# Low part of the dense activations ahead of the next split, and constant products between the steps of the routers' choice

## The reference

```python
def swiglu(h, w_gate_up, w_down):
    g, u = jnp.split(h @ w_gate_up, 2, axis=-1)
    return (jax.nn.silu(g) * u) @ w_down

def moe_swiglu(h, w_router, b_router, w_gate_up, w_down):
    ...
    logits = (hf @ w_router).astype(jnp.float32) + b_router.astype(jnp.float32)
    top_v, top_i = lax.top_k(logits, TOP_K)
    top_w = jax.nn.softmax(top_v, axis=-1)
    gates = jnp.sum(jax.nn.one_hot(top_i, N_EXPERTS, dtype=jnp.float32) * top_w[..., None], axis=1)
    ...
```

## Time and profile before

| | |
|---|---|
| median of 3 runs | 1820.67 us (1820.63 to 1828.91) |
| profiled execution | 1822.73 us |
| its span, first to last instruction | 1821.2 us |
| mean granted TensorE clock | 0.978 of full speed |
| PE busy | 1734.4 us, 95% |
| DVE busy | 1278.9 us, 70% |
| ACT busy | 998.8 us, 55% |
| POOL busy | 246.8 us, 14% |
| first dense layer | about 155 to 358 us |
| second dense layer | about 1050 to 1241 us |
| routers' choice | about 491 to 500 us and 1387 to 1396 us |

### The profile page before, as it was taken

The page is one execution under the profiler, slowest core; times in us unless marked ns, Lnnn a source line. Parts: engine busy times, 40 slices in busy tenths (PEclk is TensorE's granted clock), DMA queues, the critical chain, the costliest instruction groups (busy, mean ns, idle before and its releaser), DMA issues. The chain is left out here.

```text
span 1821.2 us, 26440 instructions
## 1 busy us (share of the span) xinstructions
PE 1734.4 (95%) x10773; PEld 1594.1 (88%) x10773; DVE 1278.9 (70%) x1245; ACT 998.8 (55%) x883; POOL 246.8 (14%) x294
## 2 busy tenths in 40 slices
PE   7989999899899999999999999999988999999997
PEld 7969899789789999999878999998976999999996
DVE  5567888774569888888866454446425788888887
ACT  5364343333457777777644354334463777777774
POOL 4838950000000000000210000000020000000010
PEclk9999999989999999999999999999998999999999
DMA  7526786654269998998943045444513799999984
GB/s 290 206 76 246 254 284 216 231 215 151 106 237 360 353 368 353 347 350 356 383 149 139 35 182 195 144 174 176 194 47 117 277 343 365 354 367 353 363 353 175
DMA packets 53756, 450.12 MB, mean 247 GB/s; under 512 B 6768, under 2 KB 8976, under 8 KB 16928
## 3 DMA queue, kind: packets, MB, share of 16 engines
q1 hardware_dynamic: 48480, 430.40, 62.4%
q0 software_dynamic: 5184, 18.40, 2.7%
HBM read 427.67 MB, written 21.10 MB: 246 GB/s over the span
## 5 line engine op out<-in xcount | busy, mean ns | idle before, releaser
L365 DVE TENSOR_TENSOR wlo<-raw,whi 128x3072 fp32r<-128x3072 f32 (+1 forms) x278 | 854.6, 3077 | 299.5 <-ACT whi L358 298.7
L358 ACT ACTIVATE whi<-raw 128x3072 fp32r<-128x3072 f32 (+1 forms) x278 | 706.2, 2541 | 412.0 <-PE PS L315 398.6
L313 PE MATMUL PS<-wlo,hT_hi 128*128 128x384 f32 (+2 forms) x1936 | 627.5, 324 | 6.2 <-DVE hT_lo L1976 3.4
L314 PE MATMUL PS<-whi,hT_lo 128*128 128x384 f32 (+2 forms) x1936 | 624.3, 322 | 0.0
L315 PE MATMUL PS<-whi,hT_hi 128*128 128x384 f32 (+2 forms) x1936 | 624.3, 322 | 0.0
L313 PEld LDWEIGHTS PS<-wlo,hT_hi 128*128 128x128 f32 x1936 | 367.4, 190 | 12.1 <-DVE hT_lo L1976 4.1
L314 PEld LDWEIGHTS PS<-whi,hT_lo 128*128 128x128 f32 x1936 | 367.4, 190 | 3.2 <-issue 0.2
L315 PEld LDWEIGHTS PS<-whi,hT_hi 128*128 128x128 f32 x1936 | 367.4, 190 | 0.3
L313 PE MATMUL PS<-wlo,mhi 128*128 128x512 f32 x352 | 143.7, 408 | 2.4 <-DVE mlo L1989 2.4
L315 PE MATMUL PS<-whi,mhi 128*128 128x512 f32 x352 | 139.1, 395 | 0.0
L314 PE MATMUL PS<-whi,mlo 128*128 128x512 f32 x352 | 139.1, 395 | 0.0
(11 more groups left out here) (372 smaller groups left out, 2021.3 us busy)
## 6 DMA issues: line engine op xcount, KB each, us to landing
raw<-in_weights SPq DMA_DIRECT2D x203, 1536.0 KB, 7.2
raw<-in_weights SPq DMA_DIRECT2D x73, 1024.0 KB, 6.2
raw<-s_tables SPq DMA_DIRECT2D x8, 1536.0 KB, 7.5
expert_rows<-ysb POOLq DMA_DIRECT2D x14, 512.0 KB, 6.8
s_tables<-g_out SPq DMA_DIRECT2D x8, 640.0 KB, 3.8
t_af<-s_rows_af SPq DMA_DIRECT2D x32, 128.0 KB, 3.8
s_tables<-g_out SPq DMA_DIRECT2D x8, 512.0 KB, 4.6
raw<-in_weights SPq DMA_DIRECT2D x3, 1152.0 KB, 5.5
```

Of the source, the lines that this page charges most:

```text
L313: pe.matmul(o, sh, mlw, start=start, stop=False, skip_group_check=True)
L314: pe.matmul(o, sl, mh, start=False, stop=False, skip_group_check=True)
L358: act.activation(whi[p0 % SPL][:, 0:n], raw[p0 % RAW][:, 0:n], ACT.Copy).then_inc(hi_done, 1)
L365: dve.tensor_tensor(wlo[p0 % SPL][:, 0:n], raw[p0 % RAW][:, 0:n], whi[p0 % SPL][:, 0:n].bitcast(F32), ALU.subtract).then_inc(lo_done, 1)
```

## The change

In `dense_act`, ScalarE makes the high part of the last activations ahead of its last split (piece u7 + 3) instead of behind it. In `dense_dve`, VectorE makes the low part of step j - 1 at the head of step j, ahead of the split of piece g + 3 instead of behind it, and at the end of the layer ahead of the split of piece u7 + 3 and of the last taps. The taps of the other steps keep their place. In `moe_pe`, TensorE issues two constant products into bank 1 behind the transposes of the logits, and one behind the counts.

```diff
@@ -1021,37 +1021,43 @@
                         .then_inc(f_hi, 1)
                 if 2 <= j < JD:
                     split_hi(act, b0 + ND["d", j - 2] + SPL)
-                if j < JD:
+                if j < JD - 1:
                     split_hi(act, b0 + ND["u", j] + SPL)
+                elif j == JD:
+                    split_hi(act, b0 + ND["u", JD - 1] + SPL)
 
         def dense_dve(dve, f, n):
             b0 = base[f"dense{f}"]
-            for j in range(JD + 2):
-                if 1 <= j <= JD:
-                    m = GU_D[j - 1][1] // P * L
-                    if j < JD:
-                        split_lo(dve, b0 + ND["g", j] + SPL)
-                    dve.wait_ge(f_hi, JD * f + j)
-                    dve.tensor_tensor(ALO[(j - 1) % 2][:, 0:m], psf[:, turn_at(j):turn_at(j) + m],
-                                      AHI[(j - 1) % 2][:, 0:m].bitcast(F32), ALU.subtract).then_inc(f_lo, 1)
-                elif j == 0:
-                    split_lo(dve, b0 + ND["g", j] + SPL)
-                if f == 0 and 1 <= j < KC:
+            def low_part(j):
+                m = GU_D[j][1] // P * L
+                dve.wait_ge(f_hi, JD * f + j + 1)
+                dve.tensor_tensor(ALO[j % 2][:, 0:m], psf[:, turn_at(j + 1):turn_at(j + 1) + m],
+                                  AHI[j % 2][:, 0:m].bitcast(F32), ALU.subtract).then_inc(f_lo, 1)
+
+            for j in range(JD):
+                if f == 0 and j >= 2:
+                    s5_taps_dve(dve, j - 1)
+                if j >= 1:
+                    low_part(j - 1)
+                split_lo(dve, b0 + ND["g", j] + SPL)
+                if f == 0 and j >= 1:
                     s5_powers_dve(dve, j)
-                if 2 <= j < JD:
+                if j >= 2:
                     split_lo(dve, b0 + ND["d", j - 2] + SPL)
-                if j < JD:
-                    p, w = b0 + ND["u", j], GU_D[j][1]
-                    dve.wait_ge(w_used, p + 1)
-                    dve.wait_ge(f_silu, JD * f + j + 1)
-                    for t in range(TT):
-                        i = dve.scalar_tensor_tensor(out=ff["act"][:, t, 0:w], in0=PS[:, 2 + t, 0:w],
-                                                     scalar=stat[:, 2, t:t + 1], in1=ff["sg"][:, t, 0:w],
-                                                     op0=ALU.mult, op1=ALU.mult)
-                    i.then_inc(f_mul, 1)
+                p, w = b0 + ND["u", j], GU_D[j][1]
+                dve.wait_ge(w_used, p + 1)
+                dve.wait_ge(f_silu, JD * f + j + 1)
+                for t in range(TT):
+                    i = dve.scalar_tensor_tensor(out=ff["act"][:, t, 0:w], in0=PS[:, 2 + t, 0:w],
+                                                 scalar=stat[:, 2, t:t + 1], in1=ff["sg"][:, t, 0:w],
+                                                 op0=ALU.mult, op1=ALU.mult)
+                i.then_inc(f_mul, 1)
+                if j < JD - 1:
                     split_lo(dve, p + SPL)
-                    if f == 0 and 1 <= j < KC:
-                        s5_taps_dve(dve, j)
+            low_part(JD - 1)
+            split_lo(dve, b0 + ND["u", JD - 1] + SPL)
+            if f == 0:
+                s5_taps_dve(dve, JD - 1)
             for half in range(2):
                 c = slice(half * 512, half * 512 + 512)
                 for t in range(TT):
@@ -1672,6 +1678,7 @@
             for t in range(TT):
                 last = pe.transpose(PS[:, 5, t * NE:(t + 1) * NE], mo["lgt"][:, t * P:(t + 1) * P], ident[0:NE, 0:NE])
             last.then_inc(m_pe, 1)
+            keep_warm(pe, 1, 2)
 
             pe.wait_ge(m_dve, 3 * m + 3)
             sel = mo["sel"]
@@ -1681,6 +1688,7 @@
                 .then_inc(m_pe, 1)
             pe.matmul(PS[:, 3, 0:NE], ones, sel[:, 0, :], start=True, stop=False, skip_group_check=True)
             pe.matmul(PS[:, 3, 0:NE], ones, sel[:, 1, :], start=False, stop=True, skip_group_check=True)
+            keep_warm(pe, 1, 1)
 
             def gather(e):
                 g = NE * m + e
```

## The result

The changed kernel took 1808.84 us, median of 7 runs (1807.88 to 1816.22), against 1820.67 us for the kernel before in 7 runs of the same comparison (1815.74 to 1828.91). The ratio is 0.9948, 95% interval 0.9925 to 0.9971, which is 9.5 us faster with 5.3 to 13.7 as the interval. The profiled execution took 1812.86 us, its span is 1811.3 us, and the mean granted clock 0.986.

The account below looks back on a forecast made before the run. TensorE, with matmuls covering 95% of the span, was taken as the bound, so only its ended stalls count: 4.5 + 2.8 + 1.0 + 0 = 8.3 us off 1820.67 gives 1812.4 us, range 1807.7 to 1817.

Parts of the forecast that it names:

- Part 1: Step 2 of the first dense layer: low part ahead of the gate split ends TensorE's idle and half-speed stretch, 4.5 us.
- no wait of TensorE for `alo` in either dense layer: Sign that the forecast is right: TensorE never waits for the activations' low part in the two dense layers.
- near 25.7 us: Sign that the forecast is right: the time from turns to turns in step 2 of the first dense layer.
- `alo` of step 2 is done at 205.6: First dense layer: VectorE finishes the low part 1.2 us before TensorE asks, everything behind being 0.7 us later.
- rival (a): VectorE is late in the stretch shared with GpSimd; the 4.5 us shrink to nothing at worst, 1816.9 us; chance 0.15.
- Part 2: End of the first dense layer: TensorE finishes 7.4 us sooner, but VectorE's queue becomes the bound, so 2.8 us arrive.
- fourth place of the queue at 351.7: End of the first dense layer: VectorE's split ends at 347.7, its table products at 351.7, then the adds to x.
- Part 3: End of the second dense layer: TensorE's wait of 0.98 us for the low part behind one split goes, 1.0 us.
- Part 4: Constants in the routers' choice: gather at full clock, but VectorE's two splits cover it and gate piece stays low; nothing.
- Rival (b): S5 begins at the low clock after 4.6 us of idle; constants take 1.9 us more, 1814.3 us; chance 0.14.
- Rival (c): Router constants hold the clock into the first gate piece, 1.5 us twice, 1809.4 us; chance 0.12.
- Rival (d): Slower: waiting for ScalarE's high part makes VectorE the bound beside GpSimd, 1834 us at worst; chance 0.04.

Follow-up runs that it names:

- e9: Changed kernel with GpSimd making only two of its eight groups of S5 tables; only times up to 350 us read: step 2 took 25.73 us.
- e3: Kernel before with the new order in the steps of both dense layers only, old order at the ends, no constants: 1815.49 us, ratio 0.9991.
- e4: Kernel before with the new order at the ends of both dense layers only, old order in the steps, no constants: 1814.73 us, ratio 0.9976.
- e8: Changed kernel with the first dense layer's last table products behind the adds to x, their store behind two table loads: 1809.51 us, ratio 0.9937.
- e2: Kernel before with only the three constant calls of each router added: 1820.97 us, ratio 1.0001.
- e1: Changed kernel without its constant calls in the routers: 1810.55 us, ratio 0.9953 to the kernel before.
- e5: Changed kernel run again without an edit: 1810.89 us, ratio 0.9947 to the kernel before.
- e10: Changed kernel with four more constant calls behind the transposes of expert 0's tokens: 1807.54 us, ratio 0.9938 to the kernel before.
- e12: Changed kernel without its own three constant calls, but with four behind the transposes of expert 0's tokens: 1809.35 us, ratio 0.9952.
- e7: Changed kernel with the first dense layer's step 1 table products moved behind the low part of step 2: 1812.14 us, ratio 0.9951.
- e6: Changed kernel with five more constant calls ahead of the norm behind the first dense layer and four ahead of expert 0's gate product: 1808.52 us, ratio 0.9936.

## Why the prediction was right

The time came out at 1808.84 us, 3.6 us under the forecast of 1812.4. It is inside the range of 1807.7 to 1817, but 0.7 us outside the narrower one of 1809.5 to 1815 that the forecast was given for itself. The three parts were named rightly, and their sum of 8.3 us was 0.8 us too high by the traces, which would make 1813.2. That the kernel came out faster than that is no merit of the prediction: 2 us by the ratios and 4 by the medians have no part that they belong to. Whether the gain lies above 0.5% was given 0.40; both comparisons came out at 0.52% and 0.53%, too near to it to say.

**Part 1, predicted 4.5 us, measured 3.2.** The mechanism was right and the size off (of its signs, "no wait of TensorE for `alo` in either dense layer" and "near 25.7 us" in step 2 failed): the half-speed stretch went entirely, but of the idle 2.74 us only 1.6 did. The term that was mis-sized is "`alo` of step 2 is done at 205.6". It carried the table products at the length they had in the trace of before, and added 0.7 us for the new wait in step 1. That 0.7 us was right: the powers start at 190.65 - 1.58 = 189.1 on the scale of before, where they started at 188.4. Then powers, split and taps grew beside GpSimd, the taps most, from 4.9 to 6.5 us, and `alo` was done at 208.54 + 0.94 - 1.58 = 207.9, 2.3 us later than predicted. I had asked whether `alo` grows, and answered that correctly (0.94). (The window of the earlier trace rows that it gave for GpSimd at work begins at 210.4, behind the split and `alo`; the trace of before has GpSimd busy beside both all the same, in one product from 205.49 to 209.23.) I hadn't asked whether what stands ahead of `alo` grows. That is rival (a) in part, at 1.3 of its 4.5 us; e9 shows its cause.

**Part 2, predicted 2.8 us, measured 3.1.** By its own steps: `alo` waited only for ScalarE's high part, VectorE became the bound, its adds ran back to back. They were expected in the fourth place of the queue at 351.7 on the scale of before and stood at 350.01 + 1.60 = 351.6. SyncE's store went out at 351.7 on that scale, as predicted near 351.8, and hid. e3 and e4 show that this gain belongs to the order at the end, and e8 that VectorE is the bound.

**Part 3, predicted 1.0 us, measured 1.2.** No wait for `alo` is left at the end of the second layer.

**Part 4, predicted nothing, measured nothing.** e2 has 1.0001 and e1 about the gain of the whole. The steps were as foreseen: the gather at full clock, VectorE's splits covering it, the gate product 8.67 us behind `pick` instead of 8.68, the first gate piece at 0.50. What costs time in expert 0 is the low clock over the gate piece. About 3.4 us of it give 33.7 to 33.9 us from `pick` to `pick` (before, first layer; e5, second layer) and some 6.8 us give 35.0 to 35.2 (changed kernel, both layers; e1, first layer) against 32.3 without. In the profiled execution the first expert layer is 1.4 us longer than before for that reason, and e1 shows that the same comes about without constants.

**Rival (b)** came true in small: in the changed kernel the clock was low from 354.5 to 361.7, the constants ahead of S5 took 3.18 us instead of 1.88, and S5's first products came 6.60 us behind the turns instead of 5.94. That costs 0.7 us, not the 1.9, because 1.40 us of waiting stood behind the constants before. The first products themselves ran at full clock (2.13 us, 2.70 before). **Rival (c)** fell: with the second gap open, no profile came to the 32.3 us from `pick` to `pick` that a layer takes without low clock. The Trainium skill, "TensorE: Matmul & The Clock Gate", section Why this matters for your kernels, advises against idle gaps between bursts; e10 agrees with it at 32.3 us once both gaps are filled, and e2 and e12 show no sure gain from filling one of two. **Rival (d)** fell: no wait for `act` appeared.

**What makes the rest.** Parts 1 to 3 sum to 7.5 us by distances; the ratios say 9.5 (5.3 to 13.7) and 9.6 (6.9 to 12.4). The 2 us between lie inside the intervals. They may be clock in stages that the change leaves alone, or chance. In thirteen profiles (e9 left out) S5 took 119.0 to 126.8 us: 126.00 before, 126.79 in e7, 122.7 in e2 and e6, 119.6 in both profiles of the changed kernel, 125.32 in e12, which is the same kernel up to and through S5, and 118.95 in e3, whose start of S5 has the old order. I find no rule in the edits for it. Whether the changed kernel on average keeps more clock in S5 than the one before stays open; telling it would take profiles of many executions of each.

## What to carry to other kernels

When an instruction is moved to the head of a queue, look at what still stands ahead of it and who runs beside that: the bound came not from the moved instruction but from the table products before it, which GpSimd slows. A stall that ends uncovers the next bound, so price a removed wait by the queue that is late next: 7.4 us of TensorE's time gave 3.1. Where two idle gaps stand ahead of a burst, filling one alone won nothing here, so test them together, and see that the filling does not itself end late (e12). Ask first whether the half-speed stretch lies over work that something else covers: clearing it from there wins nothing, as with the gather.

## What the runs showed of the hardware

- GpSimd's table work stretched VectorE's 512-element products with both operands in SBUF from 0.69 us to anything up to 2.04, and a 3072-column split from 3.36 to 4.70, while instructions that read one operand from PSUM kept their 0.94 to 0.96 and 1.13 us. The size of the growth was not expected: three times for a single instruction. GpSimd pays too: a product of 0.40 us took 3.52 beside a split.
- Half-speed stretches come and go from one execution to the next in stages with the same instructions: S5 at 119.63 us with a clock of 0.97 and at 126.79 with 0.92. The kernel before alone spread over 1812 to 1829 us. The distance of step 2, in contrast, was 27.08 to 27.12 us in the eight profiles that have its order, which is why distances carry the argument here.
- Filling the second gap alone left the clock low in the gather of both expert layers, and in the second layer also in the first 1.4 us of the filling (eight records took 4.25 us instead of 3.60); the clock was back at 1.00 for the rest of it.
